# Five more weight pairs of the input projection as seven block products, placed between the heads' preparation

## The chip, the cores and the metric

The kernel runs on one core of one Trainium2 chip. A core has a matmul engine (TensorE, PE in the profile), a vector engine (VectorE, DVE), an activation engine (ScalarE, ACT), a general engine (GpSimd, POOL) and a queue engine (SyncE, SP) that starts most of the DMAs. Each engine works through its own instruction list in order; semaphores hold an instruction until work on another engine is done. The metric is the device time of one launch in microseconds (us), lower is better.

## The reference, cut to what matters

One step of a hybrid decoder layer on 288 tokens (256 of a prompt, 32 of eight samples), all in float32. The part that is changed is the first big product, and what follows it at once:

```python
h = rmsnorm(x, norm1_w)                                   # 288 x 1024
proj = einsum('btd,de->bte', h, w_in)                     # 1024 -> 6672 columns
u_pool, u_qkv, b_raw, a_raw, z, gate_pool, gate_delta = split(proj)
q, k, v = silu(causal_conv(u_qkv))                        # 8 heads of 128
decay = exp(where(causal, G_i - G_j, -inf)); A = (k beta) k^T * decay * strict
t_inv = inverse(I + A)                                    # per head and chunk
...                                                       # chunked scan gives o
o = rmsnorm(o) * silu(z)
merged = sigmoid(gate_pool) * branch_pool + sigmoid(gate_delta) * branch_delta
```

Behind it stand two branch products, the output product and a routed mixture of 32 experts, whose weights are most of the bytes that are read.

## The kernel before

Weights of `w_in` come in 26 items of 1 MB, each for two chunks of 128 output columns: items 0 to 11 are q, k and v, 12 and 13 the pooling input, 14 to 17 the eight chunks of z, 18 to 25 the sixteen gate chunks. All orders are written out by hand; each engine's program is one function of the file.

There are two ways to compute an item. **Plain** (`proj`): for each of its two chunks eight float32 matmuls of 128x128 weights against 288 tokens, which the profile counts as sixteen MATMUL records; ScalarE then takes the bank out with Silu (z) or Tanh (gates). **Seven block products** (`late_products`, `late_products_back`): weights and tokens are cut in halves, and seven products of four matmuls against 144 tokens replace eight. The constants P1, P6, P5, P7, P3, P4, P2 name them in the order in which TensorE does them. All use banks `ps[0]` and `ps[1]` in turn, so that each waits until the result of the one two places ahead was added up: ScalarE copies P1 out (`late_first`), VectorE adds the others (`late_u2` after P6, `late_u4` after P5, `late_u7` after P7, `late_c12` after P3, `late_c21` after P4, `late_c11` after P2), each 128x144 from a bank and a tile in SBUF. P2 waits for `late_c12`, and the next pair's P1 for `late_c11`. The left sides are sums of weight blocks, which GpSimd makes in four instructions of 128x512 (`sum_weights`, s1 to s4); there is one room for them, so s1 of a pair waits for P7 of the pair ahead. The right sides are sums of token blocks, made once.

Items 1 to 11 use a form of this with more banks, and items 21 to 25 (gates 6 to 15, `LEAD_PAIR`, `PAIR_A` to `PAIR_D`) the one just told. Items 14 to 20 are plain: z0 and z1 in the pooling stage, then z2 to z7 and gates 0 and 1, each followed by `prep` of one head, then gates 2 to 5.

`prep(h)` prepares head h. TensorE makes its two products k k^T and q k^T. VectorE adds the causal mask to a table of decays (`Dt`, L2753), ScalarE takes three Exps (`rows_exp`), VectorE multiplies a second table by the result (L2757), scales the products (four at L2761) and multiplies q (L2764). Between the heads VectorE and TensorE also work through the samples' small matrices (`sample_decay`, `sample_masked`, `sample_inverse`, `sample_keys`), and GpSimd copies sample columns (`own_columns`, L907; it first waits for a DMA that writes zeros to `x_image`). After the last head the 16x16 diagonal blocks of A go out to DRAM and come back turned, VectorE inverts them in 30 small steps (L2916, L2918), they go out and in again, and TensorE merges them into full inverses (`inner_y` first), with items 21 to 25 in between.

## Time and profile before

| | |
|---|---|
| median of 3 runs | 570.27 us (568.22 to 570.81) |
| the profiled execution: its own time | 569.31 us |
| its span in the profile | 567.5 us |
| TensorE busy | 528.8 us, 93% of the span |
| VectorE / ScalarE / GpSimd busy | 291.0 / 155.6 / 166.1 us |
| TensorE's granted clock, mean | 0.983 |
| z2 starts / `PAIR_A` begins | 134.84 us / 206.78 us from the span's start |

The profile is one execution, with times counted from the span's start. A row of the timeline gives start, duration, engine, line of the kernel, operation, output and input, count; in brackets stands how long the engine had been idle before and what released it. Matmuls overlap, so the cost of a group of matmuls is the distance to the start of the next group, which is a little less than its duration.

### The profile page before, as it was taken

The numbers are of one execution on the slowest core, as the hardware profiler recorded it, in microseconds if no ns is written. First come the engines' busy times: TensorE is split into PE (matmuls) and PEld (weight loads), VectorE is DVE, ScalarE is ACT, GpSimd is POOL, SyncE is SP. The second block draws the span as 40 slices with busy tenths as digits, with TensorE's granted clock in tenths as the row PEclk, the third lists the DMA queues.
The fourth block names the chain that finished last, engine by engine and source line by source line (L and its number), as shares of the span: only waits on it lengthen the run. The fifth ranks groups of instructions, "written<-read, shape, count | busy, mean of one in ns | idle before, by whom it ended". The sixth has DMA issues, their size and how long they took to land.

```text
span 567.5 us, 13134 instructions
## 1 busy us (share of the span) xinstructions
PE 528.8 (93%) x5276; PEld 409.9 (72%) x5276; DVE 291.0 (51%) x843; ACT 155.6 (27%) x415; POOL 166.1 (29%) x247
## 2 busy tenths in 40 slices
PE   7999999999999999999999999999999949699983
PEld 6899999977777787998899888657455425365442
DVE  3877667683645848456756344533524411405044
ACT  3258466414862012233100124210011101010114
POOL 6687678113051199644033222000000000000001
PEclk9999999999999999999999999999999969889999
DMA  9835454566982138694479898899999999999992
GB/s 264 238 102 155 147 162 150 180 208 230 319 226 79 11 99 264 195 304 131 154 236 366 335 423 314 345 424 419 421 419 420 419 422 422 419 419 422 422 364 86
DMA packets 81375, 158.03 MB, mean 278 GB/s; under 512 B 11182, under 2 KB 65083, under 8 KB 69251
## 3 DMA queue, kind: packets, MB, share of 16 engines
q1 hardware_dynamic: 76572, 153.56, 73.7%
q10 hardware_dynamic: 4743, 3.64, 2.5%
q8 instruction: 42, 0.69, 0.5%
q14 instruction: 18, 0.15, 0.1%
HBM read 149.40 MB, written 7.96 MB: 277 GB/s over the span
## 4 chain that ended last, share of the span: by engine, by line
PE 73%; DMA 11%; SPq 6%; DVE 4%; issue 4%; ACT 1%; ACTq 0%; DVEq 0%
PE ps L1552 14%; PE ps L1545 12%; DMA arena<-in_w_up_dram 8%; PE ps L1874 6%; PE ps L2265 5%; PE ps L2119 5%; PE ps L2071 5%; SPq L733 4%; PE ps L2175 3%; PE ps L1498 3%; PE ps L2326 3%; PE ps L2026 2%; DMA arena<-in_w_down_dram 2%; PE ps L2346 2%; PE ps L2172 1%
## 5 line engine op out<-in xcount | busy, mean ns | idle before, releaser
L1545 PE MATMUL ps<-arena 128*128 128x288 f32 x320 | 81.4, 409 | 0.7 <-DVE arena L2516 0.7
L1552 PE MATMUL ps<-arena 128*128 128x144 f32 x616 | 78.3, 287 | 0.0
L1552 PEld LDWEIGHTS ps<-arena 128*128 128x128 f32 x616 | 76.3, 190 | 2.4 <-issue 1.9
L2265 PE MATMUL ps<-arena 128*32 128x256 f32 x1024 | 63.1, 403 | 14.8 <-DMA arena<-in_w_up_dram 13.0
L1545 PEld LDWEIGHTS ps<-arena 128*128 128x128 f32 x320 | 59.7, 190 | 17.2 <-issue 1.7
L2265 PEld LDWEIGHTS ps<-arena 128*32 128x32 f32 x1024 | 36.6, 116 | 39.3 <-issue 23.0
L997 POOL TENSOR_TENSOR arena<-arena 128x512 f32<-128x512 f32 x2 | 2.5, 1274 | 204.4 <-ACT arena L1458 204.4
L2541 DVE SCALAR_TENSOR_TENSOR ps<-arena,ps 128x312 f32<-128x312 f32 x72 | 39.1, 545 | 2.2 <-ACT ps L1117 0.9
L1874 PE MATMUL ps<-arena 128*128 128x144 f32 x280 | 37.0, 290 | 0.3 <-issue 0.3
L1874 PEld LDWEIGHTS ps<-arena 128*128 128x128 f32 x280 | 34.9, 190 | 1.7 <-issue 1.4
L1498 PE MATMUL ps<-arena 128*128 128x128 f32 (+7 forms) x162 | 26.7, 284 | 7.2 <-DVE arena L3320 5.1
L2175 PE MATMUL ps<-arena 128*128 128x128 f32 x256 | 32.3, 279 | 0.7 <-DVE arena L3298 0.6
L2175 PEld LDWEIGHTS ps<-arena 128*128 128x128 f32 x256 | 29.8, 192 | 3.6 <-issue 2.5
L2119 PE MATMUL ps<-arena 128*128 128x256 f32 x128 | 31.0, 385 | 0.0
L1498 PEld LDWEIGHTS ps<-arena 128*128 128x128 f32 (+7 forms) x162 | 18.9, 149 | 14.8 <-issue 6.4
L2071 PE MATMUL ps<-arena 128*128 128x144 f32 x224 | 27.9, 286 | 0.2 <-DVE arena L3138 0.2
L2071 PEld LDWEIGHTS ps<-arena 128*128 128x128 f32 x224 | 27.6, 190 | 0.6 <-DVE arena L3138 0.5
L3320 DVE TENSOR_TENSOR arena<-arena,ps 128x256 f32<-128x256 f32 x8 | 3.4, 421 | 48.0 <-issue 32.8
L3336 DVE TENSOR_TENSOR arena<-arena,ps 128x512 f32<-128x512 f32 (+1 forms) x35 | 21.6, 633 | 9.0 <-PE ps L2346 9.0
L2326 PE MATMUL ps<-arena 128*32 128x512 f32 x224 | 25.5, 595 | 0.5 <-ACT arena L1382 0.5
L2119 PEld LDWEIGHTS ps<-arena 128*128 128x128 f32 x128 | 23.1, 190 | 3.0 <-issue 0.4
L828 POOL TENSOR_TENSOR arena<-arena 128x512 f32<-128x512 f32 x16 | 20.4, 1272 | 8.4 <-PE ps L1874 5.2
(453 smaller groups left out, 844.1 us busy)
## 6 DMA issues: line engine op xcount, KB each, us to landing
arena<-in_w_gate_dram SPq DMA_DIRECT2D x32, 1024.0 KB, 12.5
arena<-in_w_up_dram SPq DMA_DIRECT2D x32, 1024.0 KB, 17.7
arena<-in_w_down_dram SPq DMA_DIRECT2D x28, 1024.0 KB, 17.8
arena<-in_w_in_dram SPq DMA_DIRECT2D x26, 1024.0 KB, 5.7
out_dram<-arena SPq DMA_DIRECT2D x9, 512.0 KB, 5.3
arena<-in_w_branch_delta_dram SPq DMA_DIRECT2D x4, 1024.0 KB, 10.4
arena<-in_w_out_dram SPq DMA_DIRECT2D x4, 1024.0 KB, 5.4
arena<-in_state_delta_dram SPq DMA_DIRECT2D x7, 512.0 KB, 8.2
```

Of the source, the lines that this page charges most:

```text
L733: sp.dma_start(slots[s].rearrange("p (a n) -> p a n", a=2)[:, row, cols], src.rearrange("(p a) n -> p a n", a=2)[:, row, cols]).then_inc(S ...
L1498: return nc.tensor.transpose(out, in_, ident[0:m, 0:m])
L1545: last = mm(ps[n % 2][:, 0:T], w[:, k, P * (n % 2):P * (n % 2) + P], hT[:, k, :], start=(k == 0), stop=(k == KD - 1))
L1552: last = mm(to[:, 0:HT], left[:, k, :], right[:, k, :], start=(first and k == 0), stop=(k == HK - 1), skip_group_check=True)
L1874: last = mm(ps[bank][:, 0:HT], left[:, k, :], right(k), start=(opens and k == 0), stop=(k == HK - 1), skip_group_check=True)
L2071: last = mm(bank[:, 0:HT], left[:, k, :], right[:, k, :], start=(first and k == 0), stop=(k == HK - 1), skip_group_check=True)
L2119: last = mm(bank[:, 0:256], merged[:, k, P * t:P * t + P], w[:, k, :], start=(k == 0), stop=(k == KD - 1))
L2175: ins = mm(to, x2p[:, t, k, :], G[:, t, :], start=(first and k % 4 == 0), stop=(last_tile and k % 4 == 3), skip_group_check=True)
L2265: last = mm(to[CAP * e:CAP * e + CAP, 0:FE], xgT[:, k, CAP * e:CAP * e + CAP], w[e][:, k, :], start=(k == 0), stop=(k == KD - 1))
L2326: last = mm(ps[5 + half][CAP * e:CAP * e + CAP, :], actT[:, c, CAP * e:CAP * e + CAP], w[:, c, 512 * half:512 * half + 512], start=(c == 0 ...
L2541: ins = V.scalar_tensor_tensor(c, e[:, j:j + NACC], smallT[:, NQKV * j + n:NQKV * j + n + 1], c, ALU.mult, ALU.add)
L3336: V.tensor_tensor(v, v, bank[:, 0:v.shape[1]], ALU.add).then_inc(S["m_yadd"], 1)
```

## The change

Items 15 to 19 (z2 to z7, gates 0 to 3) become seven-product pairs: `PREP_PAIRS` (15 to 18) with two heads each between their products, and `LAST_PREP` (19) behind the last head. Gates 4 and 5 (item 20) stay plain. What goes with it:

- The pairs use the token sums that items 1 to 11 used (`summed`); VectorE no longer makes them a second time (`sum_tokens` is gone). ScalarE copies them aside for the last five pairs (`token_sums`), since gates 8 to 15 are written over them.
- z2 to z7 are stored raw, and one Silu over all of them comes at the end of the stage. Before, a Silu for each chunk stood between the Exps of two heads.
- GpSimd makes twenty more weight sums, four a pair, and makes those of the lead pair a little earlier.
- VectorE makes thirty more adds (six a pair). `prep` is cut into `prep_times`, `prep_decays` and `prep_products`, with the adds in between.
- Items 12 and up use five weight slots in place of six. The zero write of `x_image` is issued two items earlier, ahead of the state loads.
- `new_values` comes before the inverse in place of behind it; `inner_y(0)` comes behind the lead pair, `inner_y(1)` inside `PAIR_A`.

```diff
+PLAIN = IN_ITEMS - 6
+PREP_PAIRS = range(PLAIN - 5, PLAIN - 1)
+LAST_PREP = PLAIN - 1
+LATE_FAST = (*PREP_PAIRS, LAST_PREP, *range(PLAIN + 1, IN_ITEMS))
...
 # gpsimd
+            sum_weights(PREP_PAIRS[0])
             nc.gpsimd.memset(X, 0.0).then_inc(S["memsets"], 1)
...
             row_masks()
             nc.gpsimd.memset(XT, 0.0).then_inc(S["memsets"], 1)
+            sum_weights(PREP_PAIRS[1])
             pool.wait_ge(S["diag"], 16)
             own_columns(0)
+            sum_weights(PREP_PAIRS[2])
             pool.wait_ge(S["sd_pe"], 1)
             own_columns(1)
-            sum_weights(LATE_FAST[0])
+            sum_weights(PREP_PAIRS[3])
+            sum_weights(LAST_PREP)
...
 # scalar
-            for h in range(H):
-                rows_exp(h)
...
-                evac(N_Z + Z_AHEAD + h)
+            for i in PREP_PAIRS:
+                h = 2 * (i - PREP_PAIRS[0])
+                late_first(i)
+                rows_exp(h)
+                rows_exp(h + 1)
...
+            act.wait_ge(S["sums"], late_added(PREP_PAIRS[2], L_SUM1))
+            nc.scalar.activation(zT[:, Z_AHEAD:H, :], zT[:, Z_AHEAD:H, :], ACT.Silu).then_inc(S["silu"], 1)
+            late_first(LAST_PREP)
...
 # tensor
-            for h in range(H):
-                proj(N_Z + Z_AHEAD + h)
-                prep(h)
+            for i in PREP_PAIRS:
+                h = 2 * (i - PREP_PAIRS[0])
+                late_products(i)
+                prep(h)
...
+                late_products_back(i)
+                prep(h + 1)
...
             state_products(1)
+            late_products(LAST_PREP)
+            sample_tiles(7, 0, P, TTq, lambda own, j: Rq[own, j, :])
+            late_products_back(LAST_PREP)
+            proj(2 * PLAIN)
+            sample_tiles(8, 2 * P, P, aqq, lambda own, j: vnq[own, j, :])
+            proj(2 * PLAIN + 1)
...
 # vector
-            for h in range(H):
-                prep(h)
+            for i in PREP_PAIRS:
+                h = 2 * (i - PREP_PAIRS[0])
+                if h:
+                    prep_times(h)
+                late_u2(i)
+                if h:
+                    prep_decays(h)
+                late_u4(i)
+                late_u7(i)
+                if h == 0:
+                    prep_times(h)
+                    prep_decays(h)
+                if h == 2:
+                    sample_masked()
+                prep_products(h)
+                late_c12(i)
+                prep_times(h + 1)
+                late_c21(i)
...
+                prep_decays(h + 1)
+                late_c11(i)
+                prep_products(h + 1)
...
-            sum_tokens()
             sample_values()
+            late_u2(LAST_PREP)
+            late_u4(LAST_PREP)
+            late_u7(LAST_PREP)
+            new_values()
+            late_c12(LAST_PREP)
+            late_c21(LAST_PREP)
+            late_c11(LAST_PREP)
```

The order of the instructions at three places follows. On TensorE, the second pair of heads (2 and 3) before: two plain chunks of eight matmuls (L1545), each followed by a head's products (L1713).

```order
L1545 MATMUL ps0<-arena 128x288 x8
L1713 MATMUL ps5<-arena 128x256 x2
L1737 MATMUL ps7<-arena 32x32 x8
L1545 MATMUL ps1<-arena 128x288 x8
L1713 MATMUL ps6<-arena 128x256 x2
```

And the same place now (L1797 is a block product, L1744 a head's products, L1768 a sample step):

```order
L1797 MATMUL ps0<-arena 128x144 x4
L1797 MATMUL ps1<-arena 128x144 x4
L1797 MATMUL ps0<-arena 128x144 x4
L1797 MATMUL ps1<-arena 128x144 x4
L1744 MATMUL ps5<-arena 128x256 x2
L1797 MATMUL ps0<-arena 128x144 x4
L1797 MATMUL ps1<-arena 128x144 x4
L1797 MATMUL ps0<-arena 128x144 x4
L1744 MATMUL ps6<-arena 128x256 x2
L1768 MATMUL ps7<-arena 32x32 x8
```

Four products now come before the first head, three before the second, and each alternates the same two banks.

On VectorE, the first of these two heads before (L2753 mask, L2757 decays, L2761 and L2764 products, L2793 a sample step):

```order
L2753 TENSOR_TENSOR arena<-arena 128x256
L2757 TENSOR_TENSOR arena<-arena 128x256 [waits expd]
L2761 SCALAR_TENSOR_TENSOR arena<-ps5,sc,arena 128x128 [waits qk_pe,dve_chain]
L2761 SCALAR_TENSOR_TENSOR arena<-ps5,sc,arena 128x128 x3
L2764 TENSOR_TENSOR arena<-arena 128x128 [waits dve_chain]
L2793 COPY arena<-ps7 128x64 [waits dec_pe]
```

And now (L2855 are the adds of the pair; L2821 to L2827 is `sample_masked`, which stood with head 1 before; L2787, L2794, L2802 and L2805 are the head's steps; the middle of `sample_masked` is left out):

```order
L2787 TENSOR_TENSOR arena<-arena 128x256
L2855 TENSOR_TENSOR arena<-arena,ps1 128x144 [waits proj_free,proj]
L2794 TENSOR_TENSOR arena<-arena 128x256 [waits expd]
L2855 TENSOR_TENSOR arena<-arena,ps0 128x144 [waits sums,proj,dve_chain]
L2855 TENSOR_TENSOR arena<-arena,ps1 128x144 [waits sums,proj]
L2821 TENSOR_TENSOR arena<-arena 128x64 [waits dec_act]
L2822 TENSOR_TENSOR arena<-arena,sc 128x64 [waits dve_chain]
...
L2827 TENSOR_TENSOR arena<-arena 128x64 [waits dve_chain]
L2802 SCALAR_TENSOR_TENSOR arena<-ps5,sc,arena 128x128 [waits qk_pe]
L2802 SCALAR_TENSOR_TENSOR arena<-ps5,sc,arena 128x128 x3
L2805 TENSOR_TENSOR arena<-arena 128x128 [waits dve_chain]
L2855 TENSOR_TENSOR arena<-arena,ps0 128x144 [waits proj]
```

The fourth add of the pair, the one for which P2 waits on TensorE, stands behind `sample_masked` and the whole of the head's products.

On GpSimd, from the clearing of `XT` on (L913), before: the copies of sample columns (L907), and one set of weight sums (L828 to L835, for the lead pair).

```order
L913 MEMSET arena 128x2048
L907 COPY arena<-arena 128x8x4 [waits diag]
...
L907 COPY arena<-arena 128x8x4 [waits sd_pe]
...
L828 TENSOR_TENSOR arena<-arena 128x512 [waits proj,ring_in3]
...
L835 TENSOR_TENSOR arena<-arena 128x512 [waits pads]
L920 MEMSET arena 128x1024 [waits sd_pe]
```

And now, the first row of each set of twelve copies (L917), and the first of each set of four sums (L837):

```order
L923 MEMSET arena 128x2048
L837 TENSOR_TENSOR arena<-arena 128x512 [waits proj,ring_in4]
...
L917 COPY arena<-arena 128x8x4 [waits diag]
...
L837 TENSOR_TENSOR arena<-arena 128x512 [waits proj,ring_in0]
...
L917 COPY arena<-arena 128x8x4 [waits sd_pe]
...
L837 TENSOR_TENSOR arena<-arena 128x512 [waits proj,ring_in1]
...
L837 TENSOR_TENSOR arena<-arena 128x512 [waits proj,ring_in2]
...
L933 MEMSET arena 128x1024 [waits sd_pe]
```

The fourth pair's sums (`ring_in1`) are queued behind the second set of copies, which waits for `state_products(0)` on TensorE (`sd_pe`).

## Rows read from the trace of the kernel before

**Rows 1.** The page, busy time, share of the span and instructions of each engine.

```profile
PE 528.8 (93%) x5276; PEld 409.9 (72%) x5276; DVE 291.0 (51%) x843; ACT 155.6 (27%) x415; POOL 166.1 (29%) x247
```

**Rows 2.** Windows from z2 to `PAIR_A`: each engine's busy time, clock, DMA share, GB/s.

```profile
134.84:184.20 49.36, 49.36 (x410) 38.17 (x408) 24.59 (x77) 28.39 (x49) 13.91 (x32) 1.00 0.77 231
184.20:207.80 23.60, 23.11 (x275) 19.01 (x273) 17.43 (x51) 2.30 (x6) 10.94 (x8) 1.00 0.14 22
```

**Rows 3.** Timeline of TensorE: head 0's sample products, two plain chunks, heads' products.

```profile
139.68 0.53 PE L1724 MATMUL ps<-arena 32*32 32x192 f32 x8
...
140.50 4.15 PE L1545 MATMUL ps<-arena 128*128 128x288 f32 x16
144.48 1.03 PE L1713 MATMUL ps<-arena 128*128 128x256 f32 x4
145.35 4.04 PE L1545 MATMUL ps<-arena 128*128 128x288 f32 x16
149.23 1.03 PE L1713 MATMUL ps<-arena 128*128 128x256 f32 x4
```

**Rows 4.** Timeline of TensorE: block products (L1874) of the late pairs.

```profile
197.65 1.25 PE L1874 MATMUL ps<-arena 128*128 128x144 f32 x8
199.15 5.16 PE L1874 MATMUL ps<-arena 128*128 128x144 f32 x40 [0.25 <-issue]
204.24 0.75 PE L1812 MATMUL ps<-arena 32*32 32x32 f32 x64
...
206.78 4.19 PE L1874 MATMUL ps<-arena 128*128 128x144 f32 x32
210.90 0.75 PE L1823 MATMUL ps<-arena 32*32 32x32 f32 x64
...
226.30 3.23 PE L1874 MATMUL ps<-arena 128*128 128x144 f32 x24
229.46 1.15 PE L1858 MATMUL ps<-arena 64*64 64x64 f32 x32
```

**Rows 5.** Timeline of VectorE and ScalarE: the first head.

```profile
139.39 0.43 DVE L2753 TENSOR_TENSOR arena<-arena 128x256 f32<-128x256 f32 x1 [8.25 <-DMA arena<-rows_image]
139.85 0.31 ACT L1158 ACTIVATE arena<-arena 128x128 f32<-128x128 f32 x1 [3.00 <-DVE arena L2753]
...
140.78 0.43 DVE L2757 TENSOR_TENSOR arena<-arena 128x256 f32<-128x256 f32 x1 [0.96 <-ACT arena L1161]
141.24 1.13 DVE L2761 SCALAR_TENSOR_TENSOR arena<-ps,sc,arena 128x128 f32<-128x128 f32 x4
142.40 0.29 DVE L2764 TENSOR_TENSOR arena<-arena 128x128 f32<-128x128 f32 x1
```

**Rows 6.** Timeline of VectorE: first and last of the seven steps of `sample_masked`.

```profile
146.99 0.22 DVE L2780 TENSOR_TENSOR arena<-arena 128x64 f32<-128x64 f32 x1
...
148.52 0.23 DVE L2786 TENSOR_TENSOR arena<-arena 128x64 f32<-128x64 f32 x1
```

**Rows 7.** Timelines of GpSimd and VectorE: weight sums of the lead pair beside head 5.

```profile
168.40 1.27 POOL L830 TENSOR_TENSOR arena<-arena 128x512 f32<-128x512 f32 x1
169.62 1.32 POOL L831 TENSOR_TENSOR arena<-arena 128x512 f32<-128x512 f32 x1
...
169.03 0.79 DVE L2764 TENSOR_TENSOR arena<-arena 128x128 f32<-128x128 f32 x1
```

**Rows 8.** Timelines of GpSimd and VectorE: sample columns beside head 5.

```profile
162.90 3.32 POOL L907 COPY arena<-arena 128x32 f32<-128x32 f32 x12 [2.14 <-PE ps L1749]
...
163.90 0.43 DVE L2757 TENSOR_TENSOR arena<-arena 128x256 f32<-128x256 f32 x1 [0.96 <-ACT arena L1161]
```

**Rows 9.** Groups by line: the adds of the late pairs, all 30.

```profile
L2828 DVE TENSOR_TENSOR arena<-arena,ps 128x144 f32<-128x144 f32 x30 | 9.1, 303 | 14.5 <-PE ps L1874 14.0
```

**Rows 10.** Timeline of VectorE: the inverse's first step, and what follows its last.

```profile
187.27 0.29 DVE L2911 TENSOR_SCALAR arena<-arena 128x256 f32<-128x256 f32 x1 [1.72 <-DMA arena<-a_image]
...
197.06 2.69 DVE L2865 TENSOR_TENSOR arena<-arena 128x1024 f32<-128x1024 f32 x1
```

More of the change, by code:

```diff
@@ L64 @@
 SUM2, SUM4, SUM7, SUM5, SUM6 = range(1, 6)
[L65 to L66 removed]
+SLOT_OF = [i % 4 for i in range(NQKV // 2)] + [0, 1, 2, 3, 4, 0, 1, 2, 3, 4, 0, 2, 3, 4, 2, 3, 0, 4, 1, 5, 2, 3, 0, 4]
+LATE_SUMMED, LATE_SUMS = 1, 5
 FIRST_DELTA = IN_ITEMS + BP_ITEMS
@@ L95 @@
 RAWN = EW - RAWC
-LEAD_GATES = 6
 Z_AHEAD = 2
@@ L111 @@
 MIX_BANK = (7, 4)
-CONV_AT = NQKV // 2 + RA
-ROWS_AT = NQKV // 2 + RA
-DIAG_AT = LATE_FAST[1]
+CONV_AT = NQKV // 2 + RA - 1
+ROWS_AT = NQKV // 2 + RA - 1
+DIAG_AT = PAIR_A
 IMAGE_FIRST = 12
@@ L824, in sum_weights @@
                 elif i in LATE_FAST:
-                    pool.wait_ge(S["proj"], product(i - 1, L_P7))
+                    pool.wait_ge(S["proj"], product(pair_ahead(i), L_P7))
                 if i - 2 in FAST:
@@ L833, in sum_weights @@
                 if i in LATE_FAST[1:]:
-                    pool.wait_ge(S["proj"], product(i - 1, L_P3))
+                    pool.wait_ge(S["proj"], product(pair_ahead(i), L_P3))
                 nc.gpsimd.tensor_tensor(s4, a12, s2, ALU.subtract).then_inc(S["pads"], 1)
@@ L1190, in _, with token_sums @@
                 read_diagonal(act, m)
-            for n in range(N_GATE + 3, N_GATE + LEAD_GATES):
-                if n == N_GATE + LEAD_GATES - 1:
-                    act.wait_ge(S["sub_done"], 1)
-                    for m in BY_SCALAR:
-                        write_inverse(act, m)
-                evac(n)
+            def token_sums():
+                act.wait_ge(S["proj"], product(PREP_PAIRS[3], L_P2))
+                at = HT * (3 * HK + 2)
+                flat_sums = summed.rearrange("p j k t -> p (j k t)")
+                nc.scalar.activation(room_l[:, 0:at], flat_sums[:, 0:at], ACT.Copy).then_inc(S["ht_done"], 1)
+                nc.scalar.activation(room_w, flat_sums[:, at:], ACT.Copy).then_inc(S["ht_done"], 1)
+            token_sums()
+            late_tanh(PREP_PAIRS[3])
+            late_tanh(LAST_PREP)
+            evac(2 * PLAIN)
+            evac(2 * PLAIN + 1)
+            late_first(LEAD_PAIR)
+            act.wait_ge(S["sub_done"], 1)
+            for m in BY_SCALAR:
+                write_inverse(act, m)
             def flat(v):
@@ L1761, in sample_flips, with late_block, late_left @@
                 last.then_inc(S["dec_pe"], 1)
+            def late_block(bank, left, right, opens=True):
+                for k in range(HK):
+                    last = mm(ps[bank][:, 0:HT], left[:, k, :], right(k), start=(opens and k == 0), stop=(k == HK - 1),
+                              skip_group_check=True)
+                last.then_inc(S["proj"], 1)
+            def late_left(i):
+                w = slots[SLOT_OF[i]].rearrange("p (k n) -> p k n", k=KD)
+                return w[:, 0:HK, 0:P], w[:, HK:KD, 0:P], w[:, HK:KD, P:2 * P]
@@ new lines, in late_right, with late_products @@
+            def late_right(i, j):
+                return (lambda k: summed[:, j, k]) if i <= LAST_PREP else lambda k: late_summed[j][k]
+            def late_products(i, between=nothing):
+                a11, a12, a22 = late_left(i)
+                s1, s2, s3, s4 = [weight_sums(i)[:, j] for j in range(4)]
+                behind_plain = i in (PREP_PAIRS[0], LEAD_PAIR)
+                pe.wait_ge(ring_in[SLOT_OF[i]], 16 * loads_in(SLOT_OF[i], i + 1))
+                if behind_plain:
+                    pe.wait_ge(S["proj_free"], free[2 * i - 2])
+                else:
+                    pe.wait_ge(S["sums"], late_added(pair_ahead(i), L_SUM1))
+                late_block(0, a11, lambda k: hT[:, k, 0:HT])
+                between()
+                pe.wait_ge(S["pads"], weights_summed(i, 2))
+                if behind_plain:
+                    pe.wait_ge(S["proj_free"], free[2 * i - 1])
+                if i == LEAD_PAIR:
+                    pe.wait_ge(S["ht_done"], late_summed_by(2))
+                late_block(1, s2, late_right(i, 1))
+                pe.wait_ge(S["proj_free"], late_free(i, 1))
+                late_block(0, s1, late_right(i, 0))
+                pe.wait_ge(S["pads"], weights_summed(i, 3))
+                pe.wait_ge(S["sums"], late_added(i, L_SUM2))
+                late_block(1, s3, late_right(i, 2))
@@ L1869, in outer_xx @@
                 last.then_inc(S["xx_pe"], 1)
-            def late_block(bank, left, right, opens=True):
-                for k in range(HK):
-                    last = mm(ps[bank][:, 0:HT], left[:, k, :], right(k), start=(opens and k == 0), stop=(k == HK - 1),
-                              skip_group_check=True)
-                last.then_inc(S["proj"], 1)
-            def late_left(i):
-                w = slots[SLOT_OF[i]].rearrange("p (k n) -> p k n", k=KD)
-                return w[:, 0:HK, 0:P], w[:, HK:KD, 0:P], w[:, HK:KD, P:2 * P]
@@ L1917, in _ @@
             late_products(LEAD_PAIR)
             late_products_back(LEAD_PAIR)
-            inner_y(1)
-            late_products(PAIR_A)
+            inner_y(0)
+            late_products(PAIR_A, lambda: inner_y(1))
             inner_xx(0)
@@ L2921, in _ @@
             ins.then_inc(S["sub_done"], 1)
-            new_values()
             spread_v()
```

136 lines of the change are left out of this document (51 added, 85 removed).

## The prediction

> **What bounds the kernel now.** The page comes first: TensorE is busy 93% of the span, every other engine far less [rows 1]. That is a mean over stages, so next come the windows of the stretch that is changed, from z2 to the first products of `PAIR_A`. In the first, 49.36 us long, TensorE is busy all of it; in the second 23.11 of 23.60 [rows 2]. So here TensorE's own work sets the end: less of it would show at once, and any new wait on it costs its whole length. Behind this stretch nothing hangs on an absolute time (the loads of the expert weights are released by the stages ahead of them), so what is won or lost here should reach the end one for one.
>
> Then the timeline of the engines that TensorE is going to wait for. VectorE is busy half of that first window and waits for ScalarE's Exps in each head; GpSimd is busy 13.91 of 49.36 us. Both have room on average. The question is whether they are in time, since block products are tied to them much more closely than plain chunks: a plain chunk needs its bank emptied by ScalarE two chunks later, a pair needs three answers from VectorE between its own products.
>
> **What TensorE saves.** Two plain chunks take 3.98 and 3.88 us, from start to start [rows 3], 7.86 together. Of a divided pair the four first products take 4.12 us (206.78 to 210.90) and the three last 3.16 (226.30 to 229.46) [rows 4], 7.28 together. That is 0.58 us a pair, 2.9 for five. The lead pair is no longer divided by `inner_y(0)`: from 197.65 to 206.78 it takes 9.13 us with a wait of 0.25 and two tile products of about 0.7, so 7.5 by itself, against at most 7.28: 0.2 more. The idle 0.49 us of the second window should go with the inverse's new place (`new_values` ahead of it): 0.5. Together **3.6 us saved**.
>
> What ScalarE, VectorE and the queues are relieved of (the Silu between the Exps, `sum_tokens`) saves nothing: TensorE waits for none of it now. What is added there costs nothing either as long as TensorE has work: ScalarE's long Silu and its copies of the token sums lie beside `state_products(1)` and the chunks of gates 4 and 5, where it is nearly free. The zero write of `x_image` lands earlier, some time around 147 us, and the state loads start two us later and are not needed before about 164.
>
> **What the new waits cost.** Two facts on VectorE and GpSimd decide this. An add of a pair takes 0.30 us [rows 9], also with GpSimd at work, since one input is in PSUM. But a step with both inputs in SBUF waits for a weight sum that is running: L2764, 0.29 us long for head 0 [rows 5], takes 0.79 for head 5, where it starts at 169.03 in the middle of a sum that ends about 169.62 [rows 7]. It then ends 0.2 us behind it. So the mask (L2753), the decays (L2757), the multiply of q (L2764) and three of the seven steps of `sample_masked` can each lose up to 1.3 us. Before, one set of four sums ran in this stage; now five do.
>
> The walk through the pairs, with the port waits in:
>
> *First pair.* P1 starts at 134.84 as before, P7 ends at 138.96. With head 0 (0.87), the sample products (139.68 to 140.50, 0.8) and two products (2.1), P2 is due at 142.75. The decay rows land at 139.39 as now [rows 5]. GpSimd starts s1 of the second pair as P7 ends, until 140.35, so the mask ends at 140.8; the Exps take 0.96; the decays wait for s2 until 141.95 and end at 142.4; products 1.16; L2764 with a short wait ends at 143.9; `late_c12` at 144.2. P2 is 1.5 late. The next mask waits for s4 until 145.1, then come Exps, decays and `late_c11`, ending about 147.4. The second pair's P1 was due at 146.2: 1.2 late. Without the port the same steps give 0.3 and 0.2.
>
> *Second pair.* P1 at 147.45, P7 ends at 151.6, P2 is due at 154.6. From 152.1 VectorE has `sample_masked`, seven steps of some 0.25 us [rows 6], ahead of the head's products. Its first step waits for s1, its second for s2, so it ends at 156.2 in place of 153.9; with 1.4 of products and the add, P2 starts at 158.0. That is 3.4 late; without the port 1.1. (If the zero write lands later than 150, s1 comes later and part of this goes to the third pair.)
>
> *Third pair.* GpSimd is early and then waits for `state_products(0)`: nothing.
>
> *Fourth pair.* GpSimd does its twelve copies (3.32 us [rows 8]) and two sums (2.6) after `state_products(0)`, 6.1 with the hand-overs. TensorE has 3.16 of products, a head, a sample step and P1, 5.4 in all. P6 is 0.7 late. VectorE then meets those late sums with its masks, and `late_u2` holds P7: 1.0, between 0 and 1.6.
>
> The copies themselves I cost at nothing on the port: the decays of head 5 start at 163.90 among them and take 0.43 as ever [rows 8]. The Trainium skill (page "SBUF — State Buffer", section "Who interferes with whom") says that a VectorE instruction with two SBUF inputs contends with any GpSimd instruction that reads SBUF, and that the loser is blocked for the whole instruction. For the weight sums the trace agrees (0.79 against 0.29 us). For the copies it shows no such wait; by the page's rule they would hold the masks of the fourth pair too and add about 0.8 us to the sum.
>
> *Gates 4.* `proj` follows `LAST_PREP`'s P2 at once and waits for `late_c11`: an add of 0.30 and the way there and back, estimated at 0.6.
>
> *Inverse and lead pair.* The steps of the inverse now find GpSimd at the lead pair's sums, which start after `LAST_PREP`'s P7 and take 5.1 us. With 9.4 for the inverse (187.27 to where `new_values` stood, 0.4 ahead of 197.06 [rows 10]), then `spread_v`, then `late_u2`, VectorE answers 16.3 us after that P7. `spread_v`'s 2.69 us is mostly a wait for GpSimd; started first it should take about 1.3 (0.43 for 256 elements and 1.1 ns for each of 768 more, from rows 5). TensorE gets to the lead pair's P7 after 15.9. That is 0.4 late. The second DMA of the diagonal blocks is then just in time.
>
> Sum of the waits: 1.5 + 1.2 + 3.4 + 0.7 + 1.0 + 0.6 + 0.4 = 8.8 us. Less the 3.6 saved, **5.2 us slower**. The profiled execution took 569.31 us, so 574.5; the median of the runs lies 0.96 higher, at 570.27, which makes **575.5 us**.
>
> **Bounds.** The waits cost nothing if VectorE answers in time everywhere: 3.6 us faster. By order alone, without the port, they cost 0.3 + 0.2 + 1.1 + 0.7 + 0 + 0.6 + 0.4 = 3.3. With every two-input step meeting the start of a sum they come to about 11.5, which is 8 us slower. I take the walk's value, since its steps follow from rows, but each depends on where a 0.4 us step falls in a 1.3 us sum.
>
> **Rivals.**
> *The port waits fall off the path, the order's waits stay.* For it: between two heads VectorE has idle time, and GpSimd waits for P7 of each pair, so that sums could start while VectorE does steps that read PSUM. Against it: those sums start exactly when the mask and `sample_masked` are due. 3.3 against 3.6: 0.3 faster, 570.0 us. Chance 0.17.
> *Faster: the answers come in time.* The late pairs of the kernel before run so: four products in 4.12 us between other work with the same waits. The one mechanism is `late_c12` and `late_c11` ending before P4 and the next head's products do, which takes 2.1 us from P7's end for the decays' end, four products and L2764. If VectorE is no more than that behind, all but GpSimd's lateness is covered, and the time is 566.7 us. Against it: the Exps alone put 0.96 us between mask and decays in each head, twice in a pair. Chance 0.13.
> *Slower, as forecast.* Chance 0.70.
>
> **How the numbers follow.** About 0.5% (2.9 us) is what a measurement of this kernel can tell from no change. The first rival lies within it, the second is faster. For the forecast's own range I take 571.5 (half the port's part) to 579.0 (the upper bound of 8 with a little room); the range that should hold the time 8 times in 10 reaches to the first rival and leaves most of the faster case out: 568.5 to 579.0. Faster 0.13, the same 0.17, slower 0.70.
>
> **What would show it.** TensorE's busy share in the first window falls from all of it to about 85%, with idle time ahead of block products that VectorE's adds release; the longest ahead of P2 in the second pair. Masks and decays of 0.8 to 1.3 us where 0.43 stood, each beside a weight sum. P6 of the fourth pair is released by GpSimd. The lead pair's first product starts some 5 us later than its 197.65. The forecast is wrong if these steps stay near 0.43, or if they are long and TensorE is not waiting; if the first decay rows land later, the first pair costs more than 1.5.

## The result, and the profile after

The changed kernel takes 575.56 us (median of 4 runs, 574.82 to 577.34), the kernel before beside it 570.34 us (4 runs). The ratio is 1.0103, 95% interval 1.0069 to 1.0138: about 1% slower, 5.2 us by the medians, as forecast. The profiled execution took 574.82 us, span 572.8; that of before 569.31 and 567.5.

First the page of the changed kernel (busy time, share and instructions by engine), which answers to [rows 1].

```profile
PE 526.8 (92%) x5396; PEld 414.1 (72%) x5396; DVE 307.6 (54%) x868; ACT 144.4 (25%) x406; POOL 191.1 (33%) x267
```

TensorE is busy 2 us less and the kernel is 5 us longer: the work fell and the waits grew by more. The windows say where. The two stretches are those of [rows 2]: from z2 to gates 2, and from there to the sixth product (P6) of `PAIR_A`.

```profile
135.03:186.12 51.09, 44.66 (x490) 39.76 (x488) 35.31 (x96) 12.68 (x33) 29.48 (x45) 0.97 0.75 230
186.12:213.81 27.69, 26.53 (x316) 23.03 (x312) 18.28 (x56) 6.86 (x14) 14.79 (x11) 1.00 0.16 30
```

TensorE was busy all of the first stretch before; now it is 44.66 of 51.09 us, which is 87%. VectorE has 35 us of busy time there in place of 25, GpSimd 29 in place of 14, and TensorE's granted clock has a mean of 0.97 where it was 1.00. The list of what TensorE waits for between 134 and 204 us (total, times, longest) names the waits:

```profile
PE ps L1797 <- DVE arena L2855: 5.8, 3, 2.9
PE ps L1714 <- DVE arena L2770: 0.7, 1, 0.7
PE ps L1797 <- POOL arena L839: 0.5, 1, 0.5
PE ps L1576 <- DVE arena L2855: 0.5, 1, 0.5
```

L1797 is a block product, L2855 an add of a pair, L839 a weight sum, L1714 the last step of the pool branch ahead of z2, L1576 a plain chunk. The timeline of TensorE shows the three waits for adds and the one for GpSimd where they stand; it answers to [rows 3, 4].

```profile
140.72 2.23 PE L1797 MATMUL ps<-arena 128*128 128x144 f32 x16
144.98 1.25 PE L1797 MATMUL ps<-arena 128*128 128x144 f32 x8 [2.03 <-DVE arena L2855]
146.07 1.03 PE L1744 MATMUL ps<-arena 128*128 128x256 f32 x4
147.14 4.16 PE L1797 MATMUL ps<-arena 128*128 128x144 f32 x32
...
157.06 2.29 PE L1797 MATMUL ps<-arena 128*128 128x144 f32 x8 [2.94 <-DVE arena L2855]
159.14 1.59 PE L1744 MATMUL ps<-arena 128*128 128x256 f32 x4
...
174.09 2.23 PE L1797 MATMUL ps<-arena 128*128 128x144 f32 x16 [0.55 <-POOL arena L839]
177.18 1.22 PE L1797 MATMUL ps<-arena 128*128 128x144 f32 x8 [0.86 <-DVE arena L2855]
...
203.10 7.63 PE L1797 MATMUL ps<-arena 128*128 128x144 f32 x56
211.27 0.75 PE L1893 MATMUL ps<-arena 32*32 32x32 f32 x64 [0.54 <-DMA arena<-x_image]
```

P2 of the first pair waits 2.03 us, P2 of the second 2.94, P6 and P7 of the fourth 0.55 and 0.86. Read two rows against each other: P2 of the second pair lasts 2.08 us to the start of the head's products (157.06 to 159.14), P2 of the first 1.09 (144.98 to 146.07). The windows around it show why: TensorE does next to nothing from 154 to 157 us, and behind that the granted clock is 0.55, most of it on the lower of the two levels, 1.2 GHz.

```profile
154.00:157.00 3.00, 0.12 (x1) 0.00 (x0) 2.79 (x13) 0.00 (x0) 2.55 (x3) 0.98 1.17 314
157.00:160.66 3.66, 3.60 (x12) 3.09 (x12) 1.29 (x5) 0.89 (x3) 0.00 (x0) 0.55 1.22 290
160.66:165.00 4.34, 4.34 (x50) 4.30 (x50) 3.15 (x11) 1.19 (x4) 0.00 (x0) 1.00 1.10 316
```

The timelines of VectorE and GpSimd show what TensorE's answers waited for. L2787 is the mask, L2794 the decays, L2805 the multiply of q, L2821 and L2822 the first two steps of `sample_masked`; L837 and L839 are weight sums, L917 is a copy of sample columns.

```profile
139.37 1.43 DVE L2787 TENSOR_TENSOR arena<-arena 128x256 f32<-128x256 f32 x1
...
143.41 1.30 DVE L2805 TENSOR_TENSOR arena<-arena 128x128 f32<-128x128 f32 x1
144.64 0.29 DVE L2855 TENSOR_TENSOR arena<-arena,ps 128x144 f32<-128x144 f32 x1
...
151.55 1.24 DVE L2821 TENSOR_TENSOR arena<-arena 128x64 f32<-128x64 f32 x1
152.83 1.31 DVE L2822 TENSOR_TENSOR arena<-arena,sc 128x64 f32<-128x64 f32 x1
154.17 0.23 DVE L2823 TENSOR_TENSOR arena<-ps,arena 128x64 f32<-128x64 f32 x1
...
170.97 0.44 DVE L2794 TENSOR_TENSOR arena<-arena 128x256 f32<-128x256 f32 x1 [0.22 <-ACT arena L1175]
```

```profile
139.26 1.26 POOL L837 TENSOR_TENSOR arena<-arena 128x512 f32<-128x512 f32 x1 [0.35 <-PE ps L1797]
...
151.44 1.27 POOL L837 TENSOR_TENSOR arena<-arena 128x512 f32<-128x512 f32 x1 [1.68 <-PE ps L1797]
152.79 1.27 POOL L839 TENSOR_TENSOR arena<-arena 128x512 f32<-128x512 f32 x1
...
168.21 3.25 POOL L917 COPY arena<-arena 128x32 f32<-128x32 f32 x12 [11.66 <-PE ps L1780]
```

The steps of [rows 5, 6] that took 0.43, 0.29 and 0.22 us take 1.43, 1.30 and 1.24 when they start beside a sum: L2821 starts at 151.55, 0.11 behind s1, and ends as s1 does; L2822 does the same with s2. The third step reads PSUM and takes 0.23 in the middle of s3. Beside the copies the decays take 0.44 [rows 8]. That is the wait of [rows 7], at its full length. The adds stay at 302 ns [rows 9].

### The profile page after: what moved, and what is told of

It reads as the page before. It is cut to its first block, busy times and chain, and to the rows that moved or that the text cites. A ratio compares the mean times of both kernels' runs of the same rounds, so it can differ in the third digit from the quotient of the medians.

```text
span 572.8 us, 13447 instructions
## 1 busy us (share of the span) xinstructions
PE 526.8 (92%) x5396; PEld 414.1 (72%) x5396; DVE 307.6 (54%) x868; ACT 144.4 (25%) x406; POOL 191.1 (33%) x267
## 4 chain that ended last, share of the span: by engine, by line
PE 66%; DMA 11%; DVE 10%; SPq 6%; issue 4%; ACT 1%; ACTq 0%; POOL 0%; DVEq 0%; POOLq 0%
PE ps L1583 13%; PE ps L1797 10%; DMA arena<-in_w_up_dram 7%; PE ps L2300 5%; PE ps L2154 5%; PE ps L2106 5%; SPq L742 4%; PE ps L2210 3%; PE ps L1527 3%; PE ps L1576 3%; PE ps L2361 3%; PE ps L2061 2%; DMA arena<-in_w_down_dram 2%; PE ps L2381 2%; PE ps L2207 1%
## 5 line engine op out<-in xcount | busy, mean ns | idle before, releaser
L1797 PE MATMUL ps<-arena 128*128 128x144 f32 x560 | 75.9, 292 | 6.6 <-DVE arena L2855 5.8
L1797 PEld LDWEIGHTS ps<-arena 128*128 128x128 f32 x560 | 71.1, 192 | 10.5 <-DVE arena L2855 5.4
L1583 PE MATMUL ps<-arena 128*128 128x144 f32 x616 | 78.3, 287 | 0.0
L1583 PEld LDWEIGHTS ps<-arena 128*128 128x128 f32 x616 | 76.3, 190 | 2.4 <-issue 1.9
L2300 PE MATMUL ps<-arena 128*32 128x256 f32 x1024 | 63.2, 404 | 14.7 <-DMA arena<-in_w_up_dram 13.3
L1011 POOL TENSOR_TENSOR arena<-arena 128x512 f32<-128x512 f32 x2 | 2.5, 1270 | 204.4 <-ACT arena L1487 204.4
L1576 PE MATMUL ps<-arena 128*128 128x288 f32 x160 | 40.5, 408 | 1.2 <-DVE arena L2551 0.7
L1576 PEld LDWEIGHTS ps<-arena 128*128 128x128 f32 x160 | 29.8, 190 | 9.4 <-issue 1.8
L2210 PEld LDWEIGHTS ps<-arena 128*128 128x128 f32 x256 | 29.8, 192 | 3.7 <-issue 2.5
L2855 DVE TENSOR_TENSOR arena<-arena,ps 128x144 f32<-128x144 f32 x60 | 18.2, 303 | 25.8 <-PE ps L1797 24.7
L837 POOL TENSOR_TENSOR arena<-arena 128x512 f32<-128x512 f32 x21 | 26.7, 1272 | 11.5 <-PE ps L1797 9.6
L2106 PE MATMUL ps<-arena 128*128 128x144 f32 x224 | 27.9, 286 | 0.2 <-DVE arena L3191 0.2
L2106 PEld LDWEIGHTS ps<-arena 128*128 128x128 f32 x224 | 27.6, 190 | 0.6 <-DVE arena L3191 0.4
L840 POOL TENSOR_TENSOR arena<-arena 128x512 f32<-128x512 f32 x21 | 27.5, 1307 | 0.0
L839 POOL TENSOR_TENSOR arena<-arena 128x512 f32<-128x512 f32 x21 | 26.8, 1277 | 1.6
```

The source lines that it names most:

```text
L837: nc.gpsimd.tensor_tensor(s1, a21, a22, ALU.add).then_inc(S["pads"], 1)
L839: nc.gpsimd.tensor_tensor(s2, s1, a11, ALU.subtract).then_inc(S["pads"], 1)
L840: nc.gpsimd.tensor_tensor(s3, a11, a21, ALU.subtract).then_inc(S["pads"], 1)
L1576: last = mm(ps[n % 2][:, 0:T], w[:, k, P * (n % 2):P * (n % 2) + P], hT[:, k, :], start=(k == 0), stop=(k == KD - 1))
L1583: last = mm(to[:, 0:HT], left[:, k, :], right[:, k, :], start=(first and k == 0), stop=(k == HK - 1), skip_group_check=True)
L1797: last = mm(ps[bank][:, 0:HT], left[:, k, :], right(k), start=(opens and k == 0), stop=(k == HK - 1), skip_group_check=True)
```

## The experiments

Each is compared with the kernel before run on the same chip. The column "z1 to lead" is from the start of z1, the last chunk that nothing here touches, to the first product of the lead pair; it leaves out what other stages do from run to run. The ratio has its 95% interval.

| kernel | ratio to before | z1 to lead, us |
|---|---|---|
| before | 1 | 67.76 |
| changed | 1.0103 (1.0069 to 1.0138) | 74.01 |
| short sums | 0.9962 (0.9937 to 0.9986) | 65.64 |
| sums as copies | 1.0000 (0.9979 to 1.0022) | 66.64 |
| `sample_masked` later | 1.0097 (1.0067 to 1.0127) | 72.23 |
| answers early | 0.9941 (0.9914 to 0.9968) | 63.74 |
| sums in four pieces | 1.0029 (1.0002 to 1.0057) | 67.97 |
| sums in eight pieces | 1.0099 (1.0065 to 1.0133) | 71.32 |
| P4 made four times | 1.0087 (1.0069 to 1.0106) | 72.41 |
| combined | 0.9922 (0.9909 to 0.9935) | 64.65 |
| combined, whole sums | 1.0044 (1.0025 to 1.0064) | 69.67 |
| combined, two pieces | 0.9996 (0.9974 to 1.0019) | 66.63 |

### Short sums

```
+                if PREP_PAIRS[0] <= i <= LAST_PREP:
+                    s1, s2, s3, s4, a11, a12, a21, a22 = [v[:, 0:1, 0:16] for v in (s1, s2, s3, s4, a11, a12, a21, a22)]
                 nc.gpsimd.tensor_tensor(s1, a21, a22, ALU.add).then_inc(S["pads"], 1)
...
```

> The changed kernel with the weight sums of z2 to z7 and of gates 0 to 3 made on 16 of their 512 columns (the other columns are left out, so these chunks are not the reference's); GpSimd's order and every wait stay. Theory (VectorE's two-input steps wait for a running weight sum): masks, decays and the steps of sample_masked go back to 0.42, 0.42 and 0.22 us; the wait of the first pair's P2 falls from 2.0 to about 0.3, that of the second pair's P2 from 2.9 to about 1.1 with the stretch at a clock of 0.56 behind it gone (1.6), the waits of the fourth pair's P6 and P7 (0.55 and 0.86) and that ahead of z2 (0.7) go: about 6 us less than the changed kernel's 575.6, 569.5 (568 to 571). Rival (the order of VectorE's steps alone makes the waits): only GpSimd's lateness at the fourth pair's P6 goes, 575.0.

566.65 us against 568.78. The mask beside the (now 0.22 us long) sums takes 0.46, the steps of `sample_masked` 0.22, and the waits ahead of z2 and of the fourth pair are gone. (The first two of these steps do not meet a sum at all here: they start at 150.65 and 150.90, the sums at 151.79, behind copies that wait for the zero write until 148.54.) The timeline of TensorE has these waits left:

```profile
144.07 1.25 PE L1799 MATMUL ps<-arena 128*128 128x144 f32 x8 [0.25 <-DVE arena L2857]
154.04 1.25 PE L1799 MATMUL ps<-arena 128*128 128x144 f32 x8 [0.83 <-DVE arena L2857]
188.01 4.12 PE L1578 MATMUL ps<-arena 128*128 128x288 f32 x16 [0.49 <-DVE arena L2857]
```

These are the order's own: 0.25, 0.83 and 0.49. Everything between 74.01 and 65.64, 8.4 us, went with the sums' length. The rival by which the order of VectorE's steps makes the waits falls. By the ratios that is 8 us less than the changed kernel where the expectation had 6. Its own terms add up to 7.2 (1.7, 1.8, 1.6, 1.4 and 0.7); the rest is what a wait costs beyond its idle time, told below.

### Sums as copies

```
+                if PREP_PAIRS[0] <= i <= LAST_PREP:
+                    for n, (to, by) in enumerate(((s1, a21), (s2, a11), (s3, a21), (s4, a12))):
...
+                        nc.gpsimd.tensor_copy(to, by).then_inc(S["pads"], 1)
+                    return
```

> The changed kernel with each of those weight sums turned into one GpSimd copy of a 128x512 block, which reads one SBUF operand in place of two and waits for nothing but the same TensorE products (the sums are left out, so these chunks are not the reference's). If only GpSimd's two-operand sums hold VectorE up: VectorE's steps as undisturbed, about 569.5. If any long GpSimd instruction that reads SBUF holds it up: masks and decays beside the copies last up to one copy longer, and the time lies between 570 and 575.6, by how long a copy is against the sum's 1.27 us.

568.84 us against 568.78, as before. A copy of 128x512 takes 621 ns (mean of 20) where the sum takes 1.27 us, and VectorE's steps beside it last up to 0.44 us longer. First mask, VectorE's timeline:

```profile
139.20 0.87 DVE L2793 TENSOR_TENSOR arena<-arena 128x256 f32<-128x256 f32 x1 [0.36 <-DMA arena<-rows_image]
```

So 0.87 in place of 0.43: a long GpSimd copy with one operand holds VectorE too. The time alone would not separate the two readings, since the 569.5 us of the first is 0.9985 of the 570.34 that stood beside the changed kernel; the rows do. The Trainium skill (page "SBUF — State Buffer", section "Who interferes with whom") puts a VectorE instruction with two SBUF inputs in contention with a GpSimd instruction that reads SBUF, and these copies agree. The twelve small copies of sample columns (0.21 us each) still show next to none of it: 0.44 and 0.46 beside them in the changed kernel, for 0.41 to 0.43 away from any. There the measurement decides: costing them at nothing was right.

### `sample_masked` later

```
-                if h == 2:
-                    sample_masked()
                 prep_products(h)
                 late_c12(i)
                 prep_times(h + 1)
                 late_c21(i)
+                if h == 2:
+                    sample_masked()
```

> The changed kernel with sample_masked (seven steps) moved on VectorE from ahead of head 2's products to behind late_c21 of the same pair, nothing else. Theory (sample_masked ahead of late_c12 is what holds the second pair's P2): that wait falls from 2.9 to under 0.8 us, the granted clock stays at 1.00 between 154 and 161 us, and some 1 to 1.5 us come back at the third pair's P1, since late_c11 then stands behind it: 572.5 (571 to 574). Rival (the delay only moves to late_c11 and the sample products of head 3): the third pair's P1 waits 2.5 us or more and the time stays within 0.6 us of 575.6.

573.54 us against 568.78: the ratio is that of the changed kernel. The wait moved, as the rival said, to the sample step that needs the result (L1768) and to the third pair's P1:

```profile
154.76 1.25 PE L1797 MATMUL ps<-arena 128*128 128x144 f32 x8 [0.36 <-DVE arena L2855]
155.84 1.03 PE L1744 MATMUL ps<-arena 128*128 128x256 f32 x4
158.70 0.33 PE L1768 MATMUL ps<-arena 32*32 32x32 f32 x16 [1.84 <-DVE arena L2827]
159.47 4.16 PE L1797 MATMUL ps<-arena 128*128 128x144 f32 x32 [0.44 <-DVE arena L2855]
```

0.36 + 1.84 + 0.44 = 2.64 us of idle time for 2.94, since the sums now met the multiply of q (0.85), the next mask (1.27) and the first step of `sample_masked` (1.07) in turn. The clock stayed at 1.00. The third pair's P1 itself waits 0.44, where the theory had 1 to 1.5 and the rival 2.5 or more. By the trace the stretch is 1.8 us shorter, about what the clock costs (1.6, under P4 below); the ratios do not separate the two kernels. My expectation of 3 us was wrong: moving the steps out of a sum's way put others into it.

### Answers early

Short sums, `sample_masked` later and cut to two steps, the heads' decays, products and the multiply of q on 8 columns.

> The changed kernel with what holds VectorE's answers up made short: the weight sums of the five pairs on 16 of 512 columns, sample_masked behind late_c21 and with two of its seven steps, the heads' decays on 8 of 128 columns and their products as two steps of 8 columns in place of four of 128 (the rest is left out, so the output is not the reference's). TensorE's instructions are unchanged. It measures what seven products save where nothing waits: by the sum 3.6 us less than the kernel before, 566.7 (565.5 to 568), with no idle time of TensorE over 0.5 us from z2 to the lead pair. Rival (the block products save less than the rows of the late pairs say): over 568.5 with TensorE as busy.

564.64 us against 568.78, 4.1 less where 3.6 was expected, with TensorE busy all of the time from z2 to gates 2 and one idle time of 0.49 ahead of gates 4. This is the changed TensorE program without waits, so it measures the saving. The second pair, in TensorE's timeline:

```profile
143.80 4.08 PE L1799 MATMUL ps<-arena 128*128 128x144 f32 x32
147.72 1.03 PE L1746 MATMUL ps<-arena 128*128 128x256 f32 x4
148.59 3.10 PE L1799 MATMUL ps<-arena 128*128 128x144 f32 x24
151.53 1.03 PE L1746 MATMUL ps<-arena 128*128 128x256 f32 x4
```

3.92 + 2.94 = 6.86 us. The other four, first to last, take 6.96, 7.07, 7.07 and 7.33 (the last three products of the fifth by their duration, since the wait follows them); the five together 35.29. The ten plain chunks that they replace took 39.61 in the kernel before (3.88 to 4.08 each, start to start). Saved: 4.3 us.

### Sums in four and in eight pieces

```
+                parts = 4 if PREP_PAIRS[0] <= i <= LAST_PREP else 1
+
+                def add(to, x, y, op):
+                    n = P // parts
+                    for p in range(parts):
+                        c = slice(n * p, n * p + n)
+                        ins = nc.gpsimd.tensor_tensor(to[:, :, c], x[:, :, c], y[:, :, c], op)
+                    ins.then_inc(S["pads"], 1)
```

> The changed kernel with each weight sum of the five pairs made in four pieces of 128x128 one behind the other, the same sums in the same order. If what holds VectorE up is the one running GpSimd instruction: masks, decays and steps of sample_masked beside a sum wait one piece, some 0.4 us, in place of 1.3, so about two thirds of the 8 us between the changed kernel (1.010 of before) and the kernel with short sums (0.996) come back: 0.4 to 1.0 us above before, ratio 1.000 to 1.003. If VectorE waits as long as GpSimd has sums to make, whatever their pieces: 1.010 or, with GpSimd's overhead for each piece, above.

> As the one in four pieces, in eight of 128x64. If VectorE waits one piece: waits of 0.2 to 0.3 us, but GpSimd takes longer for a set of sums, so the fourth pair's P6 and P7 wait longer than with four; ratio to before 0.998 to 1.003. If it waits for the whole set: above 1.010.

Four pieces: 569.49 against 569.02, by the ratio 0.3% above before and 0.74% better than whole sums, within the expectation. VectorE waits for the rest of one piece (some 0.47 us): its first mask takes 0.63, though GpSimd has sixteen pieces to make.

```profile
138.73 0.63 DVE L2796 TENSOR_TENSOR arena<-arena 128x256 f32<-128x256 f32 x1
```

```profile
138.62 7.45 POOL L843 TENSOR_TENSOR arena<-arena 128x128 f32<-128x128 f32 x16 [0.39 <-PE ps L1806]
```

The multiply of q takes 0.51, a step of `sample_masked` at most 0.34. In `sample_masked` the pieces are only part of the reason: its first two steps start at 149.42 and 149.67 and are over before GpSimd, late with its copies, starts the next set at 149.94. What is left comes from GpSimd itself. A set takes some 7.3 us in place of 5.1, and with its copies ahead of it GpSimd is late for the fourth pair's P6 (first row, four pieces). With eight pieces a set takes 10.4 us and P6 waits in the third pair as well (last two rows):

```profile
169.52 3.21 PE L1806 MATMUL ps<-arena 128*128 128x144 f32 x24 [1.60 <-POOL arena L843]
```

```profile
157.34 2.23 PE L1806 MATMUL ps<-arena 128*128 128x144 f32 x16 [1.38 <-POOL arena L843]
...
172.25 2.23 PE L1806 MATMUL ps<-arena 128*128 128x144 f32 x16 [2.79 <-POOL arena L843]
```

Its ratio of 1.0099 is the number that the second reading had (VectorE waits for the whole set), but the rows show another cause: VectorE's masks and decays take 0.41 to 0.66 us there, and TensorE's longest waits are for GpSimd. One step is an exception, a multiply of q in the fourth pair that waits some 0.9 us, about three pieces of 0.3:

```profile
177.96 1.23 DVE L2814 TENSOR_TENSOR arena<-arena 128x128 f32<-128x128 f32 x1
```

So "one piece" is what the other steps show, and why this one waited longer is not shown. I had sized GpSimd's own lateness too small.

### P4 made four times over

```
+            def late_block(bank, left, right, opens=True, times=1):
...
-                late_block(1, a22, late_right(i, 3), opens=False)
+                late_block(1, a22, late_right(i, 3), opens=False, times=4 if i == PREP_PAIRS[1] else 1)
```

> The changed kernel with the eighth-pass product P4 of the second pair (z4, z5) made four times over in place of once: 12 matmuls more, some 1.6 to 2.3 us of TensorE's work inside the 2.94 us in which it waits for late_c12 (what is added makes z5's values wrong). If TensorE's standing idle there brings the clock of 0.56 behind it: the granted clock stays at 1.00 from 157 to 161 us, P2 takes 1.05 and the head's products 0.96 as elsewhere, and the time is some 1.5 us less than the changed kernel's for all the work added, 1.0075 of before. If the fall has another cause: the clock falls there as before, 1.010.

(P4 is the product of eight matmul records that ends ahead of P2; no pass is meant.) Here only the clock is asked. All else is the changed kernel's; the first P2 waits 2.04 us, as there. The windows:

```profile
154.00:157.00 3.00, 3.00 (x27) 3.00 (x26) 2.79 (x11) 0.00 (x0) 2.96 (x3) 1.00 1.15 326
157.00:161.00 4.00, 4.00 (x42) 3.37 (x41) 3.04 (x12) 0.90 (x3) 0.00 (x0) 1.00 1.21 291
```

With work in the gap the clock stays at 1.00, and the stretch from z1 to the lead pair takes 72.41 us in place of 74.01: 1.6 less for three products more. So here the idle time brought the lower clock, and the lower clock cost 1.6 us. The ratio, 1.0087, points the same way, but its interval overlaps that of the changed kernel.

### Combined, and its parts

Four pieces (the lead pair's sums too), and a new order (the comments are not in the kernel):

```
+                if h == 2:
+                    sample_masked(0)         # three steps, ahead of u2 of the second pair
                 late_u2(i)
...
+                if h == 2:
+                    sample_masked(1)         # two, behind head 2's decays
                 late_u4(i)
...
                 if h == 2:
-                    sample_masked()          # seven steps
+                    sample_masked(2)         # two, ahead of head 2's products
                 prep_products(h)             # now without the multiply of q
                 late_c12(i)
+                prep_query(h)                # the multiply of q
...
             sum_weights(PREP_PAIRS[2])
+            sum_weights(PREP_PAIRS[3])
             pool.wait_ge(S["sd_pe"], 1)
             own_columns(1)
-            sum_weights(PREP_PAIRS[3])
...
-            proj(2 * PLAIN)
             sample_tiles(8, 2 * P, P, aqq, lambda own, j: vnq[own, j, :])
+            proj(2 * PLAIN)
```

> The reference's result in full, the changed kernel rearranged: the weight sums of the pairs from z2 to the lead pair in four pieces each; sample_masked in three parts between the adds of the second pair; the multiply of q behind late_c12; the fourth pair's sums ahead of the second sample columns; the last sample step ahead of gates 4. If the waits are those found, all but small ones go and the saving of the seven products stays: 566 (564.5 to 568) where before takes 569 to 570, ratio 0.993 to 0.996. If pieces hold VectorE as long as whole sums: over 1.005.

> The rearranged kernel of the combined run with the weight sums whole again (512 columns each), the reference's result in full: the new order alone. If VectorE's waits for a whole running sum decide, most of the 8 us that the short sums gave back stays lost in spite of the order: 571 to 574, ratio 1.003 to 1.008. If the order of VectorE's steps was the cause after all: as the combined run, 0.992 to 0.995.

> The same with each sum in two pieces of 128x256, the reference's result in full. If VectorE waits one piece, it lies between the combined run (four pieces, 0.992) and the one with whole sums, nearer to the first: 0.995 to 0.999; GpSimd's own time falls against four pieces, which gains only where it is late.

565.10 us against 569.02: 0.78% faster than before (interval 0.65% to 0.91%), the fastest kernel here that computes all of the reference, and a little below the 0.993 to 0.996 expected. What TensorE still waits for between 134 and 204 us:

```profile
PE ps L1806 <- DVE arena L2871: 1.0, 3, 0.6
PE ps L1902 <- DMA arena<-x_image: 0.7, 1, 0.7
```

With the same order and whole sums it is 571.14 against 569.39 (ratio 1.0044, as expected), with two pieces 567.80 (0.9996). That is a little above the 0.995 to 0.999 expected, and by the ratio not nearer to the run with four pieces than to the one with whole sums, as I had it; its interval leaves both open. So from whole sums to two pieces to four the ratio falls by 0.5% and by 0.7% with nothing else changed, and at four pieces the new order, with the lead pair's sums in pieces too, is worth 1.1% (1.0029 to 0.9922). With whole sums the order is worth 0.6% (1.0103 to 1.0044). Neither alone beats the kernel before.

## Why the prediction was right, point by point

The direction, the size and the mechanism held: 5.2 us was forecast and 5.2 measured. That they meet to the tenth is luck. Both sides of the sum were too small, the saving by 1.3 us and the waits by 2.0, so that from z1's start on the trace gives 5.9 us; and the measured 5.2 has an interval of 3.9 to 7.9. In the profiled execution z1 starts 0.80 us earlier than in that of before (129.09 against 129.89), a difference that stands since the first 12 us. In the profiles of the experiments it starts between 129.23 and 130.97, so this varies from execution to execution and is no effect of the pairs.

Between z1 and the lead pair the trace can be added up against the run with early answers. Its 63.74 us less its one wait (0.56 with the restart) is 63.2 of work; the changed kernel has 74.0, so 10.8 us of waits; the kernel before has 67.8, of which 0.23 is idle, so 4.3 us of work was saved.

**What TensorE saves: too small.** The five pairs were put at 2.9 us, 0.58 each; they save 4.3, 0.86 each. The term took a pair's cost, 7.28 us, from late pairs between small 32x32 products [rows 4]; between the heads' products the same seven take 6.86 to 7.07. The undivided lead pair and the end of the idle 0.49 us, 0.7 in the sum, gave about 0.6: the 0.23 us of idle time ahead of the lead pair, and 0.35 behind its first product, from which to the state product behind `PAIR_B`'s P4 it is 26.09 us after and 26.44 before. Together 4.9 where 3.6 stood.

**The new waits: too small as well.** The forecast had 8.8 us; 10.8 came ahead of the lead pair. The 0.5 of idle time behind it is in the 26.09 us above.

| wait | forecast, us | measured, us | idle time shown |
|---|---|---|---|
| ahead of z2 (pool branch) | none | 1.0 | 0.72 |
| first pair, P2 | 1.5 | 2.3 | 2.03 |
| second pair, P1 | 1.2 | 0.2 | none |
| second pair, P2 and the head behind it | 3.4 | 4.8 | 2.94 |
| third pair | 0 | 0 | none |
| fourth pair, P6 and P7 | 1.7 | 1.9 | 0.55 + 0.86 |
| gates 4 | 0.6 | 0.6 | 0.49 |
| inverse and lead pair | 0.4 | idle alone | 0.54, for the DMA |

"Measured" is how much later TensorE comes to the next group than in the run with early answers; for gates 4, where that run waits too, it is how much later than in the combined run, in which nothing waits there (3.70 us for the three products in place of 3.14). It is 0.1 to 0.3 more than each idle time (and 1.6 more behind the 2.94, for the clock). The 0.1 to 0.3 I put down to the overlap of matmuls, which a wait breaks once; no run takes that apart. It is also why the short sums gave back more than the idle times promised.

**The port.** It held: two-input steps of 0.43, 0.29 and 0.22 us become 0.9 to 1.4 beside a sum, and without long sums 8.4 us come back, among them the 0.55 us for which GpSimd itself was late and the 1.6 of the clock. Of the rivals, "the port waits fall off the path" (570.0) is excluded by that; the run with short sums comes closest to its case and gains 2 us (0.4%) where it had 0.3, since TensorE saves more than the sum had and GpSimd is not late there. "The answers come in time" (566.7) has its mechanism confirmed and its condition not met: where they do come in time the kernel gains 0.6%, but in the changed kernel they do not.

**What had no term.** The wait ahead of z2: the new first set of sums runs from 119.88 to 124.96 us, beside the pool branch on VectorE. The prediction took z2's start as unchanged and looked at the port only behind it. With short sums or with four pieces this wait is gone. And the lower clock behind the 2.94 us, 1.6 of the 4.8.

**What was under.** The first pair's P2: the walk gave the multiply of q "a short wait", but it started at 143.41, just behind s4 (143.31), and took 1.30. In the range, 571.5 is called half the port's part; half of 8.8 less 3.3 would make it 572.7. The measured time lies above either.

**What was over.** The second pair's P1: the next mask was to wait for s4 until 145.1, but started at 144.85 with the sums just over and took 0.41. GpSimd then waited for the zero write of `x_image` until 146.57 and held nothing up.

**Signs named ahead.** A busy share of about 85% (87%), masks and decays of 0.8 to 1.3 us beside sums (masks of up to 1.43, the decays at 0.43), the longest wait ahead of the second pair's P2 (2.94), P6 of the fourth pair released by GpSimd (0.55), the lead pair 5 us later (5.45): all but the long decays are there. Their starts fell between sums, or less than 0.2 us ahead of a sum's end (141.76 and 183.70, 0.45 each).

## What to carry to other kernels

A chunk that needs three answers between its own products is only as fast as the engine that answers, so lay the answering engine's steps beside what runs at the same time on the engine that it shares SBUF with, step by step and also in the stage ahead; an average of idle time says nothing there. A helper's long instruction is a wait for its neighbour, and cutting it into a few pieces is cheap until the pieces make the helper late itself: four was the best here, eight too many. A gap of TensorE costs more than it shows, by the restart and in one case by the clock behind it.

## What the hardware showed that I had not expected

*The lower clock.* Behind 2.94 us of idle time TensorE's granted clock was 0.55 for 3.66 us, though it had been busy from 147.14 to 154 us, up to that idle time. Behind idle times of 2.03, 1.84 and, with the new order and whole sums, 2.12 us it stayed at 1.00. It did so too behind the 2.79 us of the run with eight pieces (1.00 from 172.25 to 176), so a gap nearly as long did not bring the lower clock; what made the difference is not shown.

*Steps with one SBUF input wait too.* The prediction spoke of two inputs. In the changed kernel the inverse's first step, a TENSOR_SCALAR with one, takes 1.41 us beside the lead pair's last sum, 0.29 before [rows 10]. Small copies between the pool branch's windows do the same, and one of them, beside the last sum of the first set and the GpSimd memset behind it, waited for both:

```profile
123.80 2.94 DVE L2711 COPY arena<-U 32x32 f32<-32x32 f32 x1
```

```profile
123.70 1.26 POOL L844 TENSOR_TENSOR arena<-arena 128x512 f32<-128x512 f32 x1
124.90 1.80 POOL L889 MEMSET arena<- 128x2048 f32 x1
```

It ends at 126.74, as the memset does (126.70), where the same copy takes 0.17 elsewhere. The kernel before has the same memset, from 120.66 to 122.46, and one such copy beside it, which takes 0.16 elsewhere:

```profile
120.59 1.89 DVE L2674 COPY sc<-sc 32x14 f32<-32x14 f32 x1
```

So the trace of before already held a sign that the pool branch's copies wait for GpSimd, which the prediction did not read. The Trainium skill (page "SBUF — State Buffer", section "Who interferes with whom") counts copies and tensor_scalar among the instructions that can take the shared ports, and these rows agree.
